# Start and end of the expert stage: first chunk of sorted rows by one-hot products, and gathered rows added on TensorE

## The reference, cut to what matters

```python
h = rmsnorm(x, norm_ffn[i]).reshape(B * S, D)
x = x + hier_moe(h, ...)
...
weights = (g_w * top_p / jnp.sum(top_p, axis=-1, keepdims=True))
expert_id = grp[:, None] * MOE_EXPERTS_PER_GROUP + top_i
...
return (jax.nn.silu(xb @ w_gate[e]) * (xb @ w_up[e])) @ w_down[e]
```

## Time and profile before

| | us |
|---|---|
| median of 3 runs | 1704.66 (1700.25 to 1704.96) |
| the profiled execution, its own time | 1703.69 |
| its span, first to last instruction | 1700.7 |
| TensorE busy (matmuls) | 1462.1 |
| VectorE busy | 612.1 |
| ScalarE busy | 332.4 |
| mean granted clock of TensorE | 0.988 |

### The profile page before, as it was taken

The page is one execution under the profiler, slowest core; times in us unless marked ns, Lnnn a source line. Parts: engine busy times, 40 slices in busy tenths (PEclk is TensorE's granted clock), DMA queues, the critical chain, the costliest instruction groups (busy, mean ns, idle before and its releaser), DMA issues.

```text
span 1700.7 us, 24539 instructions
## 1 busy us (share of the span) xinstructions
PE 1462.1 (86%) x9187; PEld 926.3 (54%) x9187; DVE 612.1 (36%) x1520; ACT 332.4 (20%) x966; POOL 252.1 (15%) x296
## 2 busy tenths in 40 slices
PE   7999999999899777777777799999998777777776
PEld 3655466555666555545454455655865545455553
DVE  3145677743522221222214537523522222212125
ACT  2122377741210000000000235512100000000000
POOL 1121100000211111111113224000211111111112
PEclk9999999999999999999999899999999999999998
DMA  5214110042699999999998200451999999999996
GB/s 231 69 50 173 75 76 1 2 176 109 254 427 427 428 429 428 429 429 428 427 428 337 112 1 1 174 235 62 351 425 428 428 429 429 428 428 429 428 426 228
DMA packets 41280, 479.28 MB, mean 282 GB/s; under 512 B 11798, under 2 KB 12326, under 8 KB 23360
## 3 DMA queue, kind: packets, MB, share of 16 engines
q1 hardware_dynamic: 24688, 447.34, 62.4%
q0 software_dynamic: 15232, 26.35, 4.5%
q10 hardware_dynamic: 1296, 4.72, 0.8%
HBM read 460.01 MB, written 47.19 MB: 298 GB/s over the span
## 4 chain that ended last, share of the span: by engine, by line
PE 51%; DMA 39%; DVE 5%; issue 1%; ACT 1%; POOL 0%; DVEq 0%; SPq 0%; POOLq 0%; ACTq 0%
DMA sb_ring<-moe_w 26%; DMA sb_rows_space<-moe_w 10%; PE ps L1104 9%; PE ps L1292 7%; PE ps L1501 6%; PE ps L1113 5%; PE ps L1607 2%; PE ps L1637 2%; PE ps L1622 2%; PE ps L1334 2%; PE ps L1472 2%; PE ps L1365 2%; PE ps L1361 1%; PE ps L1445 1%; PE ps L1535 1%
## 5 line engine op out<-in xcount | busy, mean ns | idle before, releaser
L1104 PE MATMUL ps<-sb_ring,sb_x_block 128*64 128x256 f32 x2816 | 327.8, 386 | 83.1 <-DMA sb_ring<-moe_w 80.4
L1104 PEld LDWEIGHTS ps<-sb_ring,sb_x_block 128*64 128x64 f32 x2816 | 287.3, 198 | 160.4 <-issue 87.1
L714 POOL DMA_INDIRECT expert_rows<-sb_y_sb,sb_row_now x124 | 134.2, 1083 | 777.3 <-DVE sb_y_sb L1896 748.6
L1895 DVE COPY sb_row_now<-sb_row_of 128x1 uint32 (+1 forms) x124 | 19.0, 154 | 637.1 <-PE ps L1113 614.5
L1113 PE MATMUL ps<-sb_ring,sb_hidT 128*64 128x512 f32 x704 | 173.1, 613 | 29.8 <-ACT sb_hidT L817 29.8
L817 ACT COPY sb_hidT<-ps 128x128 f32<-128x128 f32 x128 | 33.9, 265 | 815.2 <-PE ps L1179 815.2
L1104 PE MATMUL ps<-sb_rows_space,sb_x_block 128*64 128x256 f32 x1280 | 148.5, 384 | 44.4 <-DMA sb_rows_space<-moe_w 44.4
L1104 PEld LDWEIGHTS ps<-sb_rows_space,sb_x_block 128*64 128x64 f32 x1280 | 132.3, 198 | 78.8 <-issue 60.3
L1292 PE MATMUL ps<-sb_xsT,sb_rows_space 128*128 128x512 f32 x256 | 114.7, 594 | 2.1 <-DVE sb_rows_space L2122 1.3
L1900 DVE TENSOR_TENSOR sb_x_block<-sb_xsT,sb_moe_gain 128x512 f32<-128x512 f32 x128 | 88.6, 692 | 25.2 <-issue 20.9
L1113 PEld LDWEIGHTS ps<-sb_ring,sb_hidT 128*64 128x64 f32 x704 | 43.0, 137 | 97.2 <-issue 50.9
(11 more groups left out here) (306 smaller groups left out, 1677.5 us busy)
## 6 DMA issues: line engine op xcount, KB each, us to landing
sb_ring<-moe_w SPq DMA_DIRECT2D x88, 3072.0 KB, 31.6
sb_rows_space<-moe_w SPq DMA_DIRECT2D x40, 3072.0 KB, 31.6
sb_xsT<-nsa_w_group SPq DMA_DIRECT2D x2, 2048.0 KB, 14.0
sb_ring<-nsa_w_group SPq DMA_DIRECT2D x2, 2048.0 KB, 8.0
sb_xsT<-nsa_w_out SPq DMA_DIRECT2D x1, 4096.0 KB, 12.5
kept_rows<-sb_rows_space SPq DMA_DIRECT2D x8, 512.0 KB, 2.6
token_rows<-sb_rows_space ACTq DMA_DIRECT2D x8, 512.0 KB, 2.6
sb_rows_space<-kept_rows SPq DMA_DIRECT2D x8, 512.0 KB, 26.9
```

The source lines that it names most:

```text
L714: pool.indirect_dma_start(out=ys_dram.rearrange("r (j n) -> (r j) n", j=2), out_offset=bass.IndirectOffsetOnAxis(ap=row_now[:, u:u + 1], a ...
L1104: last = nc.tensor.matmul(ps[j * BLOCK:(j + 1) * BLOCK, bank, 0:2 * P].rearrange("p (g n) -> p g n", g=2), x_rows[:, :, k], weights[:, 0:2 ...
```

## The change

h and hT change places in `rows_space`, so that slot 4 now lies over x and a half of hT, slot 5 over the other half of hT and h. Load 4 waits for the router's last logits where it waited for rows sent and for transposes. Load 5 waits for all rows sent, for the first chunk turned, and for gathers 1 to 3 alone.

Chunk 0 isn't gathered any more. VectorE compares `pos` of both choices with the column numbers, which gives for each tile of tokens a table of 128 by 128 that is 1 where a token stands at a place of the first chunk. TensorE multiplies h by it, 8 slices of width by 4 tiles of tokens, and the sums are the transposed chunk. The filler behind the sort is 12 products long, not 30.

Near the end of the stage expert 60 is finished before expert 61 begins. VectorE makes a diagonal of the second choice's weights for each tile (`scaled_ident`), and TensorE multiplies the second choice's gathered rows by it into the same sums as the kept results (sent_sums). VectorE's four additions of those rows are gone, and the order of what is left changes: the last expert's hidden rows come before the first addition.

```diff
-        h = rows_space[:, TILES * D:2 * TILES * D].rearrange("p (t n) -> p t n", t=TILES)
-        hT = rows_space[:, 2 * TILES * D:3 * TILES * D].rearrange("p (k n) -> p k n", k=KD)
+        hT = rows_space[:, TILES * D:2 * TILES * D].rearrange("p (k n) -> p k n", k=KD)
+        h = rows_space[:, 2 * TILES * D:3 * TILES * D].rearrange("p (t n) -> p t n", t=TILES)
...
+        first_hot = sorted_space[:, 4 * P:8 * P].rearrange("p (t n) -> p t n", t=TILES)
...
-        h_space = rows_space[:, TILES * D:2 * TILES * D]
-        hT_space = rows_space[:, 2 * TILES * D:3 * TILES * D]
+        hT_space = rows_space[:, TILES * D:2 * TILES * D]
+        h_space = rows_space[:, 2 * TILES * D:3 * TILES * D]
...
+        scaled_ident, _ = cut(scratch, 0, TILES, P)
...
                 sp.wait_ge(x_kept, 16 * TILES * (l + 1))
-                sp.wait_ge(first_rows_sent, 32 * (l + 1))
                 sp.wait_ge(h_ready, TILES * (FFN_ROWS[l] + 1))
-                sp.wait_ge(h_turned, 2 * TILES * (FFN_ROWS[l] + 1))
+                sp.wait_ge(logits_done, TILES * (l + 1))
                 expert_weights(sp, l, RING, RING).then_inc(weights_loaded[RING], 16)
-                for c in range(CHUNKS):
+                sp.wait_ge(rows_sent, 16 * TILES * (l + 1))
+                sp.wait_ge(chunk_turned, l * CHUNKS + 1)
+                for c in range(1, 4):
                     sp.wait_ge(rows_landed[c], 32 * l + 16)
                 expert_weights(sp, l, RING + 1, RING + 1).then_inc(weights_loaded[RING + 1], 16)
...
                 for c in range(CHUNKS):
-                    sp.wait_ge(rows_landed[c], 32)
+                    sp.wait_ge(rows_landed[c], 32 if c else 16)
...
-                pool.wait_ge(first_rows_sent, 32 * (l + 1))
-                pool.wait_ge(last_rows_sent, 32 * (l + 1))
-                for c in range(CHUNKS):
+                pool.wait_ge(rows_sent, 16 * TILES * (l + 1))
+                for c in range(1, CHUNKS):
...
-                        act.dma_start(h_dram[t * P:(t + 1) * P, :], h[:, t, :]).then_inc(
-                            first_rows_sent if t < 2 else last_rows_sent, 16)
+                        act.dma_start(h_dram[t * P:(t + 1) * P, :], h[:, t, :]).then_inc(rows_sent, 16)
...
                 def chunk_half(c):
                     act.wait_ge(chunk_turned, l * CHUNKS + c + 1)
+                    if c == 0:
+                        nc.scalar.copy(xsT[:, 0:P, 0:4], ps[:, CHUNK_BANK, :].rearrange("p (n k) -> p n k", k=4)
+                                       ).then_inc(xsT_act, 1)
+                        return
...
-                keep_busy(30)
+                keep_busy(12)
...
-                turn_chunk(0)
+                pe.wait_ge(first_hot_ready, l + 1)
+                pe.wait_ge(h_ready, TILES * (FFN_ROWS[l] + 1))
+                for k in range(KD):
+                    for t in range(TILES):
+                        last = nc.tensor.matmul(
+                            ps[:, CHUNK_BANK + k // 4, :].rearrange("p (n k) -> p k n", k=4)[:, k % 4, :],
+                            h[:, t, :].rearrange("p (m k) -> p k m", k=KD)[:, k, :], first_hot[:, t, :],
+                            start=(t == 0), stop=(t == TILES - 1))
+                last.then_inc(chunk_turned, 1)
                 turn_chunk(1)
...
                         down(i * SLOTS + n, n % SLOTS, i + n // SLOTS)
-                for n in range(SENT - SLOTS, SENT):
-                    if n + 1 < SENT:
-                        up(n + 1, (n + 1) % SLOTS, (n + 1) // SLOTS)
+                for n in range(SENT - SLOTS, SENT - 2):
+                    up(n + 1, (n + 1) % SLOTS, (n + 1) // SLOTS)
                     down(n, n % SLOTS, n // SLOTS)
+                n = SENT - 2
+                down(n, n % SLOTS, n // SLOTS)
+                up(n + 1, (n + 1) % SLOTS, (n + 1) // SLOTS)
+                down(n + 1, (n + 1) % SLOTS, (n + 1) // SLOTS)
...
                     for j in range(2):
                         rows = slice(j * BLOCK, (j + 1) * BLOCK)
                         last = nc.tensor.matmul(ps[:, kept_bank(t) + j, :], shares_T[rows, u, t * P:(t + 1) * P], y_sb[rows, u, :],
-                                                start=(u == 0), stop=(u == 1))
-                    if u == 1:
-                        last.then_inc(kept_done, 1)
+                                                start=(u == 0), stop=False)
+
+                def sent_sums(t):
+                    if t == 0:
+                        pe.wait_ge(scaled_ident_ready, l + 1)
+                    c = TILES + t
+                    pe.wait_ge(rows_landed[c], 32 * l + 32)
+                    for j in range(2):
+                        last = nc.tensor.matmul(ps[:, kept_bank(t) + j, :], scaled_ident[:, t, :],
+                                                y_at(c)[:, j * 512:(j + 1) * 512], start=False, stop=True)
+                    last.then_inc(kept_done, 1)
 
...
                 kept_sums(1, 1)
-                for t in range(2, TILES):
-                    for u in range(2):
-                        kept_sums(t, u)
+                kept_sums(2, 0)
+                kept_sums(2, 1)
+                for t in range(3):
+                    sent_sums(t)
+                kept_sums(3, 0)
+                kept_sums(3, 1)
+                sent_sums(3)
...
+                for t in range(TILES):
+                    step.mark(v.tensor_scalar(first_hot[:, t, :], col_no[:, :], pos[:, 0, t:t + 1], None, ALU.is_equal))
+                step.join()
+                for t in range(TILES):
+                    step.mark(v.scalar_tensor_tensor(out=first_hot[:, t, :], in0=col_no[:, :], scalar=pos[:, 1, t:t + 1],
+                                                in1=first_hot[:, t, :], op0=ALU.is_equal, op1=ALU.add))
+                step.join()
+                v.engine_nop().then_inc(first_hot_ready, 1)
...
+                    if c == 0:
+                        nc.vector.tensor_copy(xsT[:, 0:P, 4:8], ps[:, CHUNK_BANK + 1, :].rearrange("p (n k) -> p n k", k=4)
+                                              ).then_inc(xsT_dve, 1)
+                        return
...
                 dve.wait_ge(silu_done, base + SENT + 1)
                 join_hidden(0)
+                step(nc.vector.tensor_tensor(scaled_ident, ident[:, :].unsqueeze(1).to_broadcast([P, TILES, P]),
+                                             sent_wt[:, TILES:2 * TILES].unsqueeze(2).to_broadcast([P, TILES, P]), ALU.mult))
+                nc.vector.engine_nop().then_inc(scaled_ident_ready, 1)
                 if l == 0:
                     mla_tables()
                 keep_here(0)
...
                 def add_rows(t, k):
                     c = k * TILES + t
-                    dve.wait_ge(rows_landed[c], 32 * l + 32)
+                    dve.wait_ge(rows_landed[c], 32 * l + 32 if c else 16 * l + 16)
...
-                add_rows(0, 0)
                 dve.wait_ge(silu_done, base + SENT + 2)
                 join_hidden(1)
+                add_rows(0, 0)
+                keep_here(1)
+                add_kept(0)
                 add_rows(1, 0)
-                keep_here(1)
-                add_rows(0, 1)
-                add_kept(0)
-                add_rows(1, 1)
                 add_kept(1)
                 if l + 1 == LAYERS:
                     for t in range(2, TILES):
                         add_rows(t, 0)
-                        add_rows(t, 1)
                         add_kept(t)
                     return
...
                 turns[0] += 1
                 scale(n, 0)
                 add_rows(2, 0)
-                turned_half(m, 0)
-                add_rows(2, 1)
                 add_kept(2)
                 scale(n, 1)
                 add_rows(3, 0)
-                add_rows(3, 1)
                 add_kept(3)
+                turned_half(m, 0)
                 turned_half(m, 1)
                 for t in range(2, TILES):
                     scale(n, t)
```

More of the change, by code:

```diff
@@ L377, in build @@
         y_kept = sem("y_kept")
+        scaled_ident_ready = sem("scaled_ident_ready")
         rows_filled = sem("rows_filled")
@@ L421, in build @@
         inverted = sem("inverted")
-        first_rows_sent = sem("first_rows_sent")
-        last_rows_sent = sem("last_rows_sent")
         x_kept = sem("x_kept")
+        first_hot_ready = sem("first_hot_ready")
+        rows_sent = sem("rows_sent")
         moe_gain_loaded = sem("moe_gain_loaded")
```

## The result

The changed kernel takes 1716.03 us (median of 4 runs, 1715.18 to 1718.61); before, in the runs beside it, 1703.87 us. The medians differ by 12.2 us. The ratio, estimated from all the runs and not from the two medians alone, is 1.0074, 95% interval 1.0059 to 1.0089: slower, above the forecast of 1706 and above its range of 1697 to 1713. The profiled execution took 1715.18 us, with a span of 1713.4 (before 1700.7) and a mean granted clock of 0.995 (before 0.988). TensorE worked more, VectorE less; the DMA line of the page stands at 9 through both expert stages as in the earlier trace rows, and gets there a little later in both.

A forecast was written before the change was run, and what follows sets the result against it. It took the stream of expert weight loads to bound both expert stages, from load 8 on. Fronts of +3.2 and +1.9 us and ends of -0.3 and -2.3 summed to +2.5 on 1703.69, rounded to 1706, range 1697 to 1713.

The forecast's parts named there:

- Part 1, load 4: Load 4 no longer waits for rows written to DRAM; issued at 434.0 after h's last scaling, costed at nothing.
- Part 2, the products: First chunk by 32 one-hot products, 7.4 us on TensorE: expert 0 3.2 us earlier in first layer, 2.4 later in second.
- lead of load 8: Load 8's issue has slack before the load queue: a delay of expert 2 costs all but 0.4 us, 1.5 in second layer.
- The slow clock: First layer's expert 0 took 5.49 us at reduced clock; without a gap before it, it would run at full clock, 3.74.
- Part 3, the early load: Load 5 after three gathers; its packets alternate with gather rows and delay later chunks: +3.2 us first layer, +1.9 second.
- bounds of +6.8 and +4: Upper bounds on what load 5 behind three gathers costs, in us, in the first and second layer.
- The first rival: Several gather rows go per turn, so load 5 delays no chunk: sum -5.3 us, 1698.4; chance 0.28.
- starvation: Gathers slowed by load packets: chunk 4 lands at 465.3, TensorE waits in first layer; chunk 7 late in second.
- Part 4, the order: Expert 60 finished before expert 61 starts: scatter about 0.5 us earlier, TensorE pays about 2.5; counted inside the ends.
- Part 5, the ends: Second-choice additions moved from VectorE to TensorE: -2.3 us at the last layer's end, -0.3 at the first's.
- The sum: Both layers' starts and ends together: 3.2 + 1.9 - 0.3 - 2.3 = +2.5 us.
- My slower rival: Gathers starved at full price: +6.8 us first layer, +4 second, ends -2.6, 1711.9; chance 0.22.

The follow-up runs named there:

- after again: The changed kernel, unchanged, run once more beside other kernels on one chip: ratio 1.0064 (1.0046 to 1.0081) against the kernel before.
- sums in line: The changed kernel, with each first-chunk product writing 128 neighbouring numbers of PSUM instead of every fourth: products 15.48 us, ratio 1.0038 (1.0025 to 1.0051).
- strides measured: The changed kernel plus seven groups of eight unused 128x128x128 products behind the last layer's last sums, each with other operand strides; no total time given.
- before again: The kernel before, unchanged, run once more for a trace on the chip of the runs beside it: ratio 0.9993 (0.9980 to 1.0005).
- both in line: The changed kernel with first-chunk weights read from neighbouring columns and sums written to neighbouring numbers: products 7.41 us, 1711.7 us in its single run.

## Why the prediction was wrong, point by point

**Part 1, load 4: right.** Issued at 433.79 (forecast 434.0; before 433.99), so it could gain nothing.

**Part 2, the products: the step that failed.** VectorE's part was right (eight operations in 2.0 us) and so was the start, 445.42 for 445.4. The term "32 x 0.23 = 7.4 us, if other weights each time cost nothing more" was mis-sized: 15.48 us, beyond even the upper end of 10. I priced products of the right shape by a row with the right shape (L1156, the filler) and did not compare how the weights are read: the filler reads the identity in line, the products read every eighth float32. With weights in line the same products took 7.41 us. The trace of before had two signs of strides, and they point opposite ways. Transposes that read the rows with this stride (L1091, eight records in 1.08 us between 960 and 965 us, at a granted clock of 1.00) take what transposes in line take (L1264, eight in 1.09), and would have called it harmless. The weight loads of the experts would not. An expert's first products load 64 columns out of `x_block` with a stride of 8 (L1104, `x_rows[:, :, k]`), its second ones 64 columns in line (L1113); the page of before gives the mean in ns behind the busy time:

```profile
L1104 PEld LDWEIGHTS ps<-sb_ring,sb_x_block 128*64 128x64 f32 x2816 | 287.3, 198 | 160.4 <-issue 87.1
...
L1113 PEld LDWEIGHTS ps<-sb_ring,sb_hidT 128*64 128x64 f32 x704 | 43.0, 137 | 97.2 <-issue 50.9
```

That is 61 ns more for 64 columns. There it hides behind a moving operand of 256 columns (379 ns a record); for 128 columns twice that, an estimate, would have been 122, and measured are 334 against 192.

Put 8.1 us more into the working and the rest falls into place. First layer: 454.4 + 8.1 = 462.5, measured 462.58. Second: 1211.8 + 8.1, and 6.0 for the late start of the layer, 1225.9, measured 1226.02. By the lead of load 8 (0.4 and 1.5 us) the fronts then cost 6.7 - 0.4 = 6.3 and 10.6 - 1.5 = 9.1; measured 6.4 and 9.3. Load 8 itself, the number that was to decide, landed at 503.3 and 1265.1 (forecast near 501 and 1252): 5.6 us later than before in the first layer, and 8.8 in the second, counted from the layer's start.

**The slow clock: wrong in the profiled execution, right in three others.** I let expert 0 of the first layer run at full clock, since TensorE would work without a gap before it. It did, at a granted clock of 1.00 for 15 us, and the clock fell to 0.78 all the same; expert 0 took 5.42 us, before 5.49. But the same kernel in after again, first layer:

```profile
462.55 3.74 PE L1111 MATMUL ps<-sb_ring,sb_x_block 128*64 128x256 f32 x32 [0.65 <-DVE sb_x_block L1939]
```

```profile
460.00:465.00 5.00, 4.35 (x42) 3.97 (x43) 2.58 (x7) 1.17 (x2) 0.00 (x0) 1.00 0.74 248
```

The traces of sums in line and strides measured, with products of 15.48 us too, also have 3.74 us and a clock of 1.00 there. With a gathered first chunk expert 0 of the first layer took 4.73 to 5.58 us in eight traces, never 3.74. So the products mostly kept the clock up, as forecast, and what they gave back is small beside 8.1 us. A wait of 0.65 us stands before expert 0 in all four, so the wait isn't what tells them apart, and no run here says what does.

**Part 3, the early load: right in its mechanism, not in play.** Load 5 went out at 460.98, not 456.4, since its own wait for the products was the later one; all gathers were in. Where it was let loose, packets alternated as the earlier trace rows say, and it cost the kernel before 8 to 15 us in two layers, where my bounds of +6.8 and +4 make 10.8; the second layer passed its bound already in the fastest run (5.8). What I missed is the loop: TensorE waits for a chunk, so no slot comes free, so the DMA stands empty after it was too full. The first rival (gathers aren't held up), which had 0.28, is refuted by these rows. In the changed kernel itself the starvation that I charged was never put to the test. The section of the Trainium skill that spoke for the first rival (DMA: Bandwidth & Descriptors, section Queues, rings and completion order) describes packets of several descriptors; 33 to 31 packets in turn, with rows of 4 KB, disagree for gathers of this kind.

**Part 4, the order: no gain.** Forecast: the scatter leaves 0.5 us earlier. From the start of expert 60 to the scatter of expert 61 it is 19.26 us in the first layer, 19.48 before, so 0.2, and alone the order gave 1.0008, not told from nothing.

**Part 5, the ends: right.** Last layer -2.3 forecast, -2.6 in the trace; first layer -0.3 forecast, -0.4 in the trace; together -2.6 forecast, -3.2 and -2.4 us in the two timed comparisons. Full clock in the last layer's sums, as taken. In the first layer TensorE stood 4.88 us before its sums and the clock was 0.50, as forecast.

**The numbers.** The sum was 2.5; with the products' true price, expert 0 as slow as in this execution, and the starvation out of play, 6.3 - 0.3 + 9.1 - 2.3 = 12.8, measured 12.7. An agreement to 0.1 is luck: between before again and after again the same parts, each layer counted from its token indices, are 8.1, +1.4, 9.1 and -3.1, so a part of a single execution is good to 1 or 2 us. My slower rival ended on the right side for a wrong reason: it charged the gathers, and the time went into TensorE. The error of the range is the same as that of the sum: I had treated the products as an operation whose price the trace shows, when only their shape was in it, and so gave them a bound of a third where the truth was twice.

## What to carry to other kernels

Price a matmul by a row that has the same operands' strides, not only the same shape: here float32 weights read 16 or 32 bytes apart doubled the time of a 128-column product, and so did a moving operand read 32 bytes apart. A change of layout avoids it, but the stride then moves to whoever writes that layout (2051 ns for 1133 on ScalarE). A product that replaces a gather moves work from a queue that has time to the engine that bounds the stretch; even at half its price it brought nothing. A load let in before small gathers can slow the very engine whose progress issues the next loads, so bound it by the whole loop and not by the turns that it takes. And before a trace is called typical, see where its execution lies among the runs: a clock that was slow in one execution here was full in three others.

## What the runs showed of the hardware

- Strides of float32 operands of 128x128x128 products, 16 records each: 1.95 us at stride 1, 2.05 at 2, 3.90 at 4, 3.97 at 8; the moving operand 3.89 at stride 8; the written sum at stride 4 free (1.95). In the transposes of a gathered chunk (64x64) the same stride of 8 adds less: 1.10 us for 16 records with it, 0.71 without.
- Weight loads of 64 columns of float32: 198 ns at stride 8, 137 in line (means, before).
- ScalarE's scaling of 128x1024 float32, read in line and written with a stride of 128 numbers, took 2051 ns, 1133 in line.
- TensorE's granted clock fell to 0.78 right after 15 us of products at 1.00 in the first layer of one execution, and stayed at 1.00 in the same stretch of three others.
- On two chips the kernel before took some 4.5 us more than on two others, and on those, the copies of the first chunks came up to 4.8 us late during the gathers (both in line, first layer: products over at 454.6, copy at 459.4). That the one makes the other is not shown.
